# A decoder block's expert layer: gathering each token's experts, or multiplying every token by all of them

## The reference

```
q = (x @ w_query).reshape(B, T, 8, 2, 128)                # 8 heads, two half queries each
s1 = einsum('bthd,nd->bthn', q[..., 0, :], sub_keys_1)    # 128 scores
s2 = einsum('bthd,nd->bthn', q[..., 1, :], sub_keys_2)    # 128 scores
v1, i1 = top_k(s1, 16);  v2, i2 = top_k(s2, 16)
cand_s = v1[..., :, None] + v2[..., None, :]              # 256 candidates
cand_e = i1[..., :, None] * 128 + i2[..., None, :]
top_s, top_pos = top_k(cand_s, 16)
experts = take_along_axis(cand_e, top_pos)                # 16 of 16384 per token and head
g = softmax(top_s)
u = expert_down[e]
hdn = gelu(einsum('chkd,cd->chk', u, x))
y = einsum('chk,chkd->cd', g * hdn, expert_up[e])
```

## Time and profile before

| what | value |
|---|---|
| median of 3 runs | 951.32 us (950.63 to 953.27) |
| span of the profiled execution, first to last instruction | 862.9 us |
| that execution's own time | not given by the page; the median is 88.4 us above the span |
| busy: tensor engine | 755.6 us (88%) |
| busy: vector engine / GpSimd / scalar engine | 564.1 / 575.1 / 180.2 us |
| transfers | 308.39 MB, 268.47 MB of them by gathers |

### The profile page before, as it was taken

One profiled execution on the slowest core, in us unless ns is written; L12 is line 12 of the kernel. 1 busy time (PEld: TensorE's weight loads), 2 busy tenths in 40 slices (PEclk: granted clock), 3 DMA queues, 4 the chain that ended last, 5 costly groups with the idle time before them and its releaser, 6 DMA issues.

```text
span 862.9 us, 9305 instructions
## 1 busy us (share of the span) xinstructions
PE 755.6 (88%) x2473; PEld 390.9 (45%) x2473; DVE 564.1 (65%) x1503; ACT 180.2 (21%) x563; POOL 575.1 (67%) x716
## 2 busy tenths in 40 slices
PE   9999999999999879788888888888879797777786
PEld 6988668556554424244333434343434242222232
DVE  3565686239999667676767676666676666765445
ACT  2134455211212021122202030202020202112021
POOL 6886451017767777777777777777777777777770
PEclk9999999999999999999999999999999999999999
DMA  8948450659999999999999999999999999999997
GB/s 304 232 133 243 156 236 5 242 243 363 409 380 410 409 409 409 410 409 410 409 409 410 410 410 409 410 409 409 410 410 410 409 410 409 410 410 410 409 409 292
DMA packets 99487, 308.39 MB, mean 357 GB/s; under 512 B 18504, under 2 KB 23424, under 8 KB 99456
## 3 DMA queue, kind: packets, MB, share of 16 engines
q0 software_dynamic: 73728, 268.47, 78.3%
q1 hardware_dynamic: 24656, 39.39, 13.8%
q10 hardware_dynamic: 1072, 0.16, 0.1%
HBM read 306.41 MB, written 1.05 MB: 356 GB/s over the span
## 4 chain that ended last, share of the span: by engine, by line
PE 27%; DMA 27%; POOL 24%; issue 12%; DVE 8%; ACT 1%; DVEq 0%; ACTq 0%
PE bank L1530 24%; POOL region_w L647 18%; DMA region_w<-in_expert_up,chosen 14%; DMA region_w<-in_expert_down,chosen 11%; POOL gates L647 3%; DMA pool_bd<-in_expert_down,chosen 2%; PE xn_ps L1530 2%; PE bank L1533 2%; DVE region_w L1392 1%; POOL dn_spare L647 1%; POOL pool_bd L647 1%; DMA dn_spare<-in_expert_down,chosen 1%; DVE gates L1392 1%; DVE pool_bd L1392 1%; DVE region_q L1166 0%
## 5 line engine op out<-in xcount | busy, mean ns | idle before, releaser
L1530 PE MATMUL bank<-region_w,pool_bd 128*128 128x512 f32 (+2 forms) x1006 | 473.1, 598 | 96.6 <-DMA region_w<-in_expert_up,chosen 89.2
L1530 PEld LDWEIGHTS bank<-region_w,pool_bd 128*128 128x128 f32 x1006 | 174.4, 189 | 366.4 <-issue 294.5
L647 POOL DMA_INDIRECT region_w<-in_expert_up,chosen x250 | 234.8, 939 | 82.7 <-issue 61.4
L1392 DVE CUSTOM_DVE_ANT_0 region_w<-xn_ps,region_w 128x1024 f32<-128x1024 f32 x128 | 156.6, 1224 | 101.4 <-DMA region_w<-in_expert_down,chosen 101.0
L647 POOL DMA_INDIRECT region_w<-in_expert_down,chosen x128 | 120.6, 943 | 40.8 <-issue 32.9
L1392 DVE CUSTOM_DVE_ANT_0 gates<-xn_ps,gates 128x1024 f32<-128x1024 f32 x64 | 78.1, 1223 | 36.7 <-DMA gates<-in_expert_down,chosen 33.1
L908 ACT ACTIVATE pool_bd<-ident,pool_bd 128x128 f32<-128x128 f32 x251 | 78.4, 389 | 77.2 <-PE bank L1530 53.8
L647 POOL DMA_INDIRECT gates<-in_expert_down,chosen x64 | 60.4, 943 | 23.4 <-issue 16.5
L711 ACT ACTIVATE pool_bd<-bank 128x256 f32<-128x256 f32 (+3 forms) x49 | 19.0, 389 | 265.5 <-PE bank L1530 241.3
L1530 PE MATMUL bank<-region_q,oT 128*128 (+1 forms) x240 | 54.3, 379 | 0.0
L1392 DVE CUSTOM_DVE_ANT_0 dn_spare<-xn_ps,dn_spare 128x1024 f32<-128x1024 f32 x32 | 39.2, 1224 | 18.8 <-DMA dn_spare<-in_expert_down,chosen 18.6
(11 more groups left out here) (289 smaller groups left out, 786.8 us busy)
## 6 DMA issues: line engine op xcount, KB each, us to landing
region_q<-in_w_in SPq DMA_DIRECT2D x4, 2048.0 KB, 8.4
region_q<-in_w_query SPq DMA_DIRECT2D x1, 6144.0 KB, 23.9
region_w<-in_expert_up,chosen POOLq DMA_INDIRECT x250, 13.9
region_w<-in_w_out SPq DMA_DIRECT2D x1, 3072.0 KB, 20.9
x_sb<-in_x SPq DMA_DIRECT2D x4, 512.0 KB, 4.0
region_q<-in_w_in SPq DMA_DIRECT2D x2, 1024.0 KB, 11.4
region_q<-in_w_in SPq DMA_DIRECT2D x16, 128.0 KB, 3.0
region_w<-in_wb_nsa SPq DMA_DIRECT2D x2, 1024.0 KB, 16.6
```

The lines of the kernel that those rows point to most:

```text
L647: pool.indirect_dma_start(out=row, out_offset=None, in_=table, in_offset=bass.IndirectOffsetOnAxis(ap=of_slot(chosen, s, k), axis=0)).then ...
L1392: dve.tensor_tensor_reduce(out=row, in0=xn_ps[:, :], in1=row, scale=1.0, scalar=0.0, op0=ALU.mult, op1=ALU.add, accum_out=hdn[:, k:k + 1]) ...
L1530: return pe.matmul(out_, lhsT, rhs, start=start, stop=stop)
```

## The change

Every token is multiplied by every expert, and the picked ones are given their weights afterwards; all others get the weight zero. Each table is read once, in 128 blocks of 128 rows (512 KB a block), by plain transfers that SP issues.

- **Down products.** For a block, the 128 rows must lie with the width across the partitions. 75 blocks are turned on the vector engine in 32 x 32 squares (`flip`), after four transfers that place the pieces so that the squares make up the whole; 53 blocks (every fourth from block 15 to 95, and all from 96 on) come in one transfer and are turned by 8 transposes on the tensor engine (`turn_down`), copied out by the scalar engine (`turned_down`). Then 8 products with 256 columns (both tiles) give the block's hidden values (`hidden`), and the scalar engine applies the gelu to pairs of blocks (`gelu`) into one large table, experts by tokens.
- **Picks.** Queries and key scores stay as many as before; the picking (`choose`) no longer makes row numbers, it keeps both half numbers and the score of each pick. Softmax is taken once for all 16 head tiles. The tensor engine turns these three tables (`table`).
- **Weights.** For each token, a 128 x 128 table of weights over both half numbers is a product of two one-hot matrices: `one_a`, four comparisons and scalings a group of four tokens on the vector engine, and `one_b`, two comparisons on the vector engine and two on GpSimd (`hot_rows`, `hot_columns`). `weights` makes 64 groups of four such products; `weigh` multiplies a group into the hidden values that are there already, and for blocks still to come `hold` (scalar engine) stores the weights and `weigh_late` (GpSimd) or the gelu's order completes them. This starts at block 100 of the down products, two groups a block, and 8 groups are left behind block 127.
- **Up products.** For each of 128 blocks 4 products with 512 columns (`add_up`), first those of tile 0 for the first four blocks, once the weights of half the groups are in.
- **Order.** Both tiles' branch and output products come before any expert work; the norm's scale goes into the turning (`hiddenT` is 16 products with 128 columns by a scaled diagonal instead of 16 transposes). The norm and the output at the end keep their shape.

The core of the diff:

```diff
-RING = 8
-SLOTS = TOP
-STEPS = 2 * NH
+NB = NK
+RAWS, URING = 4, 8
+FIRST, SPLIT, RINGB, LATE = 12, 4, 60, 96
+GROUP_TOK = 4
+NGROUPS = TOK // GROUP_TOK
+UNITS_Q = 2 * NH
+FLIPPED = [b < FIRST or (b < LATE and b % 4 != 3) for b in range(NB)]
...
-            def gather(row, arrived, table, k, s):
-                pool.indirect_dma_start(
-                    out=row, out_offset=None, in_=table,
-                    in_offset=bass.IndirectOffsetOnAxis(ap=of_slot(chosen, s, k), axis=0)).then_inc(arrived, 16)
-            def up(n):
...
+            def load_down(b):
+                if b >= RAWS:
+                    if FLIPPED[b - RAWS]:
+                        sp.wait_ge(flipped, flipped_upto(b - RAWS))
+                    else:
+                        sp.wait_ge(turned_mm, turned_upto(b - RAWS))
+                row = raw_d[b % RAWS]
+                if not FLIPPED[b]:
+                    sp.dma_start(row, a["expert_down"][b * P:(b + 1) * P, :]).then_inc(raw_in[b % RAWS], 16)
+                    return
+                for q in range(4):
+                    sp.dma_start(row[32 * q:32 * q + 32, :].rearrange("i (g d) -> i g d", g=4),
+                                 a["expert_down"][b * P:(b + 1) * P, 256 * q:256 * q + 256].rearrange(
+                                     "(g i) d -> i g d", g=4)).then_inc(raw_in[b % RAWS], 16)
+            def load_up(b):
+                if b < RAWS:
+                    sp.wait_ge(turned_mm, turned_upto(NB - RAWS + b))
+                elif b < URING:
+                    sp.wait_ge(h_mm, NB - URING + b + 1)
+                else:
+                    sp.wait_ge(u_used, b - URING + 1)
+                sp.dma_start(u_rows[b % URING], a["expert_up"][b * P:(b + 1) * P, :]).then_inc(u_in[b % URING], 16)
...
-            def dot(k, s):
-                dve.wait_ge(dn_in[k % RING], (2 * s + k // RING + 1) * 16)
-                row = ring_dn[k % RING]
-                dve.tensor_tensor_reduce(out=row, in0=xn_ps[:, :], in1=row, scale=1.0, scalar=0.0,
-                                         op0=ALU.mult, op1=ALU.add, accum_out=hdn[:, k:k + 1]).then_inc(dn_used, 1)
+            def flip(b):
+                dve.wait_ge(raw_in[b % RAWS], raw_landed(b))
+                if slot_before(b) >= 0:
+                    dve.wait_ge(h_mm, slot_before(b) + 1)
+                dve.transpose(out=bc(dt(b)[:, 0, 0:1], [[32, 4], [P, KC], [1, 32]]),
+                              in_=raw_d[b % RAWS].rearrange("p (g j k) -> p g k j", g=4, k=KC)).then_inc(flipped, 1)
...
+            def hot_rows(g):
+                if g >= 2:
+                    dve.wait_ge(grid_mm, g - 1)
+                for n in range(GROUP_TOK):
+                    tok = GROUP_TOK * g + n
+                    last = dve.tensor_scalar(out=one_a[:, tok % 8, :], in0=iota128[:, :], scalar1=tab[:, 0, tok:tok + 1],
+                                             scalar2=tab[:, 2, tok:tok + 1], op0=ALU.is_equal, op1=ALU.mult)
+                for n in range(2):
+                    tok = GROUP_TOK * g + n
+                    last = dve.tensor_scalar(out=one_b[:, tok % 8, :], in0=iota128[:, :], scalar1=tab[:, 1, tok:tok + 1],
+                                             scalar2=None, op0=ALU.is_equal)
+                last.then_inc(hot_dve, 1)
+            def weigh(g):
+                many = gelu_before(g)
+                dve.wait_ge(grid_mm, g + 1)
+                dve.wait_ge(gelu_done, many // 2)
+                part = hw3[:, 0:many, group_tokens(g)]
+                dve.tensor_tensor(out=part, in0=part, in1=grid(g)[:, 0:many, :], op=ALU.mult).then_inc(weighed_in, 1)
...
+            def hot_columns(g):
...
+                    tok = GROUP_TOK * g + n
+                    last = pool.tensor_scalar(out=one_b[:, tok % 8, :], in0=iota128[:, :], scalar1=tab[:, 1, tok:tok + 1],
+                                              scalar2=None, op0=ALU.is_equal)
+                last.then_inc(hot_pool, 1)
+            def weigh_late(b):
...
+                for c in (b, b + 1):
+                    part = hw3[:, c, 0:GROUP_TOK * before]
+                    last = pool.tensor_tensor(out=part, in0=part, in1=temps[c % 2][:, 0:GROUP_TOK * before], op=ALU.mult)
+                last.then_inc(late_ready, 1)
...
+            def turned_down(b):
+                act.wait_ge(turned_mm, turned_upto(b))
+                act.wait_ge(h_mm, slot_before(b) + 1)
+                for half in range(2):
+                    last = copy(dt(b)[:, 4 * half:4 * half + 4, :], banks[2 + half][:, :].rearrange("p (a b) -> p a b", a=4))
+                last.then_inc(turned_cp, 1)
+            def gelu(m):
+                act.wait_ge(h_mm, 2 * m + 2)
+                early = GROUP_TOK * groups_before(2 * m)
+                both = banks[m % 2][:, :].rearrange("p (e t) -> p e t", e=2)
+                last = act.activation(hw_pair[:, m, :, early:TOK], both[:, :, early:TOK], ACT.Gelu_apprx_tanh)
...
+            def hold(g):
+                act.wait_ge(weighed_in, g + 1)
+                copy(hw3[:, gelu_before(g):NB, group_tokens(g)], grid(g)[:, gelu_before(g):NB, :]).then_inc(held, 1)
...
-            def weigh_turn(t, k, s):
-                pe.wait_ge(diag_ready, s * SLOTS + k + 1)
-                pe.wait_ge(up_in[k % RING], (2 * s + k // RING + 1) * 16)
-                for half in range(2):
-                    last = mm(banks[2 * t + half][:, :], diag[:, k, :], ring_up[:, k % RING, cols[half]], False, False)
-                last.then_inc(up_used, 1)
+            def turn_down(b):
+                pe.wait_ge(raw_in[b % RAWS], raw_landed(b))
+                if turned_upto(b) > 1:
+                    pe.wait_ge(turned_cp, turned_upto(b) - 1)
+                for k in range(KC):
+                    last = tr(banks[2 + k // 4][:, k % 4 * P:(k % 4 + 1) * P], col_chunk(raw_d[b % RAWS], k))
+                last.then_inc(turned_mm, 1)
+            def hidden(b, t=None):
...
+                for k in range(KC):
+                    last = mm(to, dt(b)[:, k, :], oTv[:, k, :] if t is None else oTv[:, k, tok_rows[t]], k == 0, k == KC - 1)
+                if t != 0:
+                    last.then_inc(h_mm, 1)
+            def weights(g):
+                pe.wait_ge(hot_dve, g + 1)
+                pe.wait_ge(hot_pool, g + 1)
+                if g >= 2:
+                    pe.wait_ge(weighed_in, g - 1)
+                    pe.wait_ge(held, held_upto(g - 2))
+                for n in range(GROUP_TOK):
+                    s = (GROUP_TOK * g + n) % 8
+                    last = mm(banks[4 + g % 2][:, n * P:(n + 1) * P], one_b[:, s, :], one_a[:, s, :])
+                last.then_inc(grid_mm, 1)
+            def add_up(b, t, half, stop=False):
+                if t == 0 and half == 0:
+                    pe.wait_ge(u_in[b % URING], 16 * (b // URING + 1))
+                return mm(banks[ffn_bank(t, half)][:, :], hw3[:, b, tok_rows[t]], u_rows[b % URING][:, cols[half]], False, stop)
...
+            for b in range(LATE, NB):
+                for c in turns_before(b):
+                    turn_down(c)
+                for g in groups_at(b):
+                    weights(g)
+                hidden(b)
+                if b == LATE + 1:
+                    for t in range(2):
+                        table(t)
+            for g in range(groups_at(NB - 1).stop, NGROUPS):
+                weights(g)
...
+            for b in range(RAWS):
+                for half in range(2):
+                    add_up(b, 0, half)
+            pe.wait_ge(weighed_in, NGROUPS)
...
```

1009 lines of the change are left out of this document (393 added, 616 removed).

## The result

The changed kernel takes **1296.87 us** (median of 4 runs, 1296.02 to 1297.03), the kernel before 952.30 (4 runs, 950.63 to 965.17): 1.361 times as long, interval 1.3575 to 1.3644. The direction was forecast; the time, 1385, was 88 us too long and the measured one lies outside the range. The profiled execution had a time of 1296.02 us and a span of 1294.3. The span was forecast at 1296.4.

The account below looks back on a forecast made before the run. Transfers were taken to bound the expert layer before, the tensor engine afterwards: 220.0 + 1054.2 + 16.9 idle + 5.3 at the end = 1296.4 us span, plus 88.4 outside it, forecast 1385 us, range 1370 to 1442.

Parts of the forecast that it names:

- 88.4 above the span: Outside the span: the runs' median 951.3 less the profiled span 862.9, kept unchanged for the changed kernel.
- The start of the expert work: End of the first part, at 220.0 us, including 3.6 for the turned, scaled rows and 1.6 of uncovered norm work.
- Dense products: Tensor engine, expert work: down products 443.3 us (3.46 a block of 256 columns), up products 439.3.
- Transfers beside them: Expert work: 134.2 MB of tables need 328 us, lying beside the tensor engine's 1054.2 us.
- Turned blocks: Vector engine before block 96: 63 blocks at 1.3 us each, priced from a dot, nothing on the path.
- threshold of 3.5 us: Rival 2's limit: from this price per turned block the vector engine bounds blocks before 96; 1458 us at 4.7, chance 0.05.
- Strided weight loads: The 424 transposes' loads, 141 ns each, assumed hidden; 60 us if shown in full, kept for the range.
- Weights' stretch: From block 100: 6.11 us a block, 2.9 a vector-engine group, then 16.9 us idle behind block 127.
- Rival 1: Weights' stretch becomes the vector engine's, at 3.9 us a group through meetings with GpSimd: 1442 us, chance 0.15.
- the meeting with GpSimd: Weights' groups: GpSimd's operations slow the vector engine's comparisons, raising a group from 2.5 to 2.9 us.
- rival 3: Clock falls under 800 us of dense matmuls; a twentieth at 1.2 GHz adds 53: 1438 us, chance 0.03.
- Rival 4: Transfers still set the time, dense products going at one record's pace instead of two: 944 us, chance 0.01.

Follow-up runs that it names:

- before_again: The kernel before, run again unchanged to read time and span of the same execution: 952.47 us (10 runs), ratio 1.0014.
- after_beside: The changed kernel with 120 extra 512 KB transfers, issued by ScalarE, meant to lie beside the up products: 1405.19 us.
- before_none: The kernel before with each of the 512 gathers replaced by a GpSimd memset of the same buffer, no row read: 732.03 us.
- before_plain_slow: The kernel before with plain transfers of neighbouring rows for gathers, each behind a waited-for memset of 500 floats on GpSimd: 912.56 us.

## Why the prediction was right and wrong

- **The step that failed** is the last one: "the median of the runs lies 951.3 - 862.9 = 88.4 above the span, and I keep that". What lies outside a span measured 1.7 us in the profile after and 2.0 in before_again. The 88 us were time inside other executions than the one profiled, which only kernels with gathers showed and the changed kernel doesn't. 1294.3 and 1.7 make the time of the profiled execution, 1296.02; by the forecast's own span, 1296.4, the time would have been 1298. The premise "nothing in it depends on the tables" had no row behind it, and its rival (the two numbers come from different executions) should have been priced, at 1298.
- **The start of the expert work**: 219.80, forecast 220.0, but with the first tile's turned rows alone. Those products of 128 columns went at 0.475 us, not 0.223 (16 records, 8 products, in some 3.8 us). Their strided weight loads took 332 ns, where those of the dense products have 190; I put the slower pace down to them, which no run tests. So the 3.6 us for both tiles were one tile's, and the second tile's 3.96 and its 0.78 us of waiting came on top. A wait of 0.78 before 184.06, behind ScalarE's copy of the merged rows, was not foreseen either.
- **Dense products**: the down products at 3.45 us a block, the up products 439.5 from their first start, 849.21, to the last eight records (1285.24 and one more piece of 3.44). Forecast 3.46 and 439.3. These terms carry the result, and they were right.
- **Transfers beside them**: right. The up products waited for none, and some 47 MB more beside them changed nothing (after_beside).
- **Turned blocks**: forecast 1.3 us, measured 2.03. The dot was the wrong neighbour; the strided copy had bounded it. At a threshold of 3.5 us it stayed hidden: the tensor engine has no wait for one.
- **Strided weight loads** of the turned blocks: 189 ns where the rows had 141, hidden as assumed: 8 transposes in 0.88 us (764.14 to 765.02). Of the 60 us in the range none was needed. Only beside the scaled rows' loads, above, was the pace slower.
- **Weights' stretch**: a late block 6.12 us, forecast 6.11. Rival 1 didn't come: the last four groups took 2.16 us each, not 2.9, so the gaps behind block 127 were 5.8 us, not 16.9. Four of six comparisons overlapped one another: 256 of 366 ns took 78.3 us busy, 0.306 each, as assumed; the meeting with GpSimd, 0.4 of the 2.9, was hardly there. Its price came from GpSimd's additions, and GpSimd's comparisons don't cost that: 0.22 at most for four. Where GpSimd did multiply, for the last of the late blocks, one group took 2.92 us (833.22 to 836.14), and its gap of 1.76 is the largest of the 5.8.
- **Clock**: from 860 us to the end 1.00, the level of 2.4 GHz (rival 3 didn't come). Only in the gaps, 840 to 845 us, was the grant 0.66 on average: 16 records with 128 columns took 3.81 us there, 1.95 at 765.02. **Rival 4** had the right fact (bytes bound the layer before; before_none) and the wrong price: a product kept the pace of two records.
- **The sum** was 1296.4 and the span 1294.3, by errors that cancel: 11.1 us too much idle time, against 4.7 for the second tile's turning, 1.9 at the lower clock and some 2 in small pieces.

## What to carry over

Before a difference between a profile's span and timed runs is carried into a forecast, look for what it could be: here the profiled span and the runs came from executions that differ by 88 us, and the changed kernel has none of that. Halving the bytes won nothing here, where the tensor engine had 15% to spare and the change gave it the dots' work in full float32: price the new work in the engine's own timeline first. Take the price of two engines' meeting from the very operations that will meet. When traffic is doubled to test a bound, put it on a queue that nobody waits for, and read the bound engine's waits, not the total.

## What was unexpected of the hardware

- The same gathering program takes 864.93 us on one chip (11 runs) and 948 to 955 (set medians) on five others, while plain transfers of the same bytes take 864.56 there. In before_again 2068 of the gathers' 65536 packets of 4 KB took over 250 ns, against 163 in the given profile. Slow packets alone aren't the loss: before_plain_slow has 1770 of them and no pause of the tensor engine over 2.7 us.
- The loss needs gathers, and a few plain transfers among them take most of it away: 884 us with an eighth of the gathers replaced, 867 with half. The long pauses all stand where the scalar engine must take over the query product.
- GpSimd's products hold up the vector engine's comparisons, by up to 0.74 us in 1.10; GpSimd's comparisons hardly do, by 0.09 on average.
- The Trainium skill ("SBUF — State Buffer", the "DVE blocks DMA" trap) says that transfers from GpSimd's queue starve while the vector engine holds the shared ports. The traces give no sign that this is the 88 us: the gathers' own durations are 939 ns in the given profile and 946 ns in before_again, they start at the same pace in both, and plain transfers from the same queue beside the same work take 864.56 us.
